# Slots in PSUM named one by one in three dense stages, and two low parts moved behind the gated output's norm

## What is computed

```
for l in range(2):
    q, k, v, r, a_low, u, v_sgu = split(x @ w_in[l])
    y_gla = gla_group(q, k, v, r, a_low, ...)      # ... * silu(r)
    y_sgu = sgu_group(u, v_sgu, ...)
    x = layer_norm(ALPHA * x + concat(y_gla, y_sgu) @ w_out[l])
    x = layer_norm(ALPHA * x + mem_xattn(x, mem, wq, wk, wv, wo))
    x = layer_norm(ALPHA * x + grouped_moe(x))     # 16 experts, 2 of them for a token
h = rms_norm(x)
proj = h @ w_in_2                                  # q, k, v, z, xbc, dt, gate_a, gate_b
y_a = moba_attention(q, k, v) @ w_out_a
u   = ssd(xbc, dt) * silu(z)
y_b = rms_norm_in_groups(u) @ w_out_b
x = x + (gate_a * y_a + gate_b * y_b) @ w_out_2
x = x + hier_moe(rms_norm(x))                      # 16 experts
x = x + sigmoid(x @ w_ple_gate) * (p @ w_ple_proj)
out = rms_norm(x)
```

## Time and profile before

| | us |
|---|---|
| median of 3 runs | 1660.1 |
| the runs | 1664.85, 1658.19, 1660.1 |
| the profiled execution | 1664.57 |
| its span, first to last instruction | 1662.8 |
| its mean granted TensorE clock | 0.966 of full speed |

### The profile page before, as it was taken

The page is one execution under the profiler, slowest core; times in us unless marked ns, Lnnn a source line. Parts: engine busy times, 40 slices in busy tenths (PEclk is TensorE's granted clock), DMA queues, the critical chain, the costliest instruction groups (busy, mean ns, idle before and its releaser), DMA issues.

```text
span 1662.8 us, 21036 instructions
## 1 busy us (share of the span) xinstructions
PE 1543.1 (93%) x8087; PEld 1296.8 (78%) x8087; DVE 1274.3 (77%) x1594; ACT 1119.2 (67%) x1340; POOL 57.2 (3%) x94
## 2 busy tenths in 40 slices
PE   7999988999997989998999998898998889999976
PEld 5788877888886778976788886787887778888855
DVE  4757458999997476447999998558655689999963
ACT  4544537999994644445999997267453479999952
POOL 5000000000001000000000000000000000000000
PEclk8999999999998999999999999999988999999988
DMA  9345427999996534534999998343533479999950
GB/s 330 124 164 202 152 102 271 391 392 392 393 395 249 173 134 170 204 125 153 377 391 393 393 395 334 121 152 102 172 132 98 162 249 388 392 393 395 394 194 26
DMA packets 176693, 422.75 MB, mean 254 GB/s; under 512 B 7052, under 2 KB 7216, under 8 KB 176576
## 3 DMA queue, kind: packets, MB, share of 16 engines
q1 hardware_dynamic: 172400, 407.92, 67.2%
q0 software_dynamic: 4176, 13.30, 2.4%
HBM read 420.15 MB, written 1.05 MB: 253 GB/s over the span
## 4 chain that ended last, share of the span: by engine, by line
PE 72%; DVE 16%; ACT 7%; issue 4%; DMA 1%; POOL 0%; POOLq 0%; ACTq 0%; DVEq 0%
PE ps L960 14%; DVE w_low L1652 11%; PE ps L986 7%; PE ps L675 5%; PE ps L676 4%; PE ps L680 4%; PE ps L997 4%; ACT w_high L1336 3%; PE ps L722 3%; PE ps L782 3%; PE ps L723 3%; PE ps L969 3%; PE ps L789 3%; PE ps L783 3%; PE ps L727 3%
## 5 line engine op out<-in xcount | busy, mean ns | idle before, releaser
L1652 DVE TENSOR_TENSOR w_low<-raw,w_high 128x1024 fp32r<-128x1024 f32 x588 | 693.9, 1222 | 253.3 <-ACT w_high L1336 250.1
L1336 ACT ACTIVATE w_high<-raw 128x1024 fp32r<-128x1024 f32 x588 | 598.2, 1055 | 334.7 <-PE ps L680 122.9
L986 PE MATMUL ps<-w_high,hT 128*128 128x512 f32 x384 | 154.0, 401 | 0.4
L986 PE MATMUL ps<-w_low,hT 128*128 128x512 f32 x384 | 153.2, 399 | 0.0
L960 PE MATMUL ps<-w_high,x_first 128*128 128x512 f32 x384 | 152.4, 397 | 0.3 <-ACT x_first L1389 0.2
L960 PE MATMUL ps<-w_low,x_first 128*128 128x512 f32 x384 | 150.2, 391 | 0.0
L675 PE MATMUL ps<-w_high,act_high 128*128 128x512 f32 x272 | 111.3, 409 | 6.4 <-DVE w_low L1652 3.6
L1652 DVE TENSOR_TENSOR w_low<-work,w_high 128x1024 fp32r<-128x1024 f32 x96 | 113.1, 1221 | 0.0
L676 PE MATMUL ps<-w_low,act_high 128*128 128x512 f32 x272 | 109.3, 402 | 0.0
L1652 DVE TENSOR_TENSOR w_low<-x_res,w_high 128x1024 fp32r<-128x1024 f32 x90 | 106.0, 1221 | 0.0
L680 PE MATMUL ps<-w_high,act_low 128*128 128x512 f32 x272 | 104.0, 395 | 0.0
(11 more groups left out here) (372 smaller groups left out, 3102.9 us busy)
## 6 DMA issues: line engine op xcount, KB each, us to landing
raw<-in_w_up SPq DMA_DIRECT2D x96, 1024.0 KB, 8.8
raw<-in_w_gate SPq DMA_DIRECT2D x51, 1024.0 KB, 9.0
raw<-in_w_down SPq DMA_DIRECT2D x48, 1024.0 KB, 8.6
work<-in_w_gate SPq DMA_DIRECT2D x45, 1024.0 KB, 8.7
x_res<-in_w_down SPq DMA_DIRECT2D x45, 1024.0 KB, 8.2
raw<-in_w_in SPq DMA_DIRECT2D x44, 1024.0 KB, 6.2
raw<-in_w_out SPq DMA_DIRECT2D x12, 1024.0 KB, 5.0
raw<-in_wk_x SPq DMA_DIRECT2D x8, 1024.0 KB, 5.0
```

Of the source, the lines that this page charges most:

```text
L986: i = pe.matmul(YS[:, b, :], hT[:, k, :], weights(u, 512 * b, 512 * b + 512)[half_w], start=(k + half_w == 0), stop=(k + half_w == FC))
L1336: A(split_unit(n)[0], raw_unit(n), ACT.Copy).then_inc(high_ready, 1)
L1652: V.tensor_tensor(split_unit(n)[1], raw_unit(n), split_unit(n)[0].bitcast(F32), ALU.subtract).then_inc(low_ready, 1)
```

## The change

The round-robin slots are replaced by named ones for the jobs from k0a to pos in each layer of the first kind, and from uT0 to pos in the last block. In a layer, s0 to s3 are the slots of mix_sgu, o0, o1 and r:

| job | slot before, layer 0 (its job before) | slot after, layer 0 (its job before) |
|---|---|---|
| k0a, k0b | 2 (o1), 3 (r) | 0 (mix_sgu), 1 (o0) |
| yT0, yT1 | 0 (mix_sgu), 1 (o0) | 2 (o1), 3 (r) |
| xva | 2 (k1a) | 2 (h0) |
| x1T0, x1T1 | 0 (h0), 1 (h1) | 3 (h1), 0 (k1a) |
| pT0, pT1 | 2 (q1b), 3 (xvb) | 0 (q1a), 1 (s0) |
| xh0, xh1 | 2 (pT0), 3 (pT1) | 0 (pT0), 1 (pT1) |
| x2T0, x2T1 | 3 (xh1), 2 (xh0) | 3 (oT0), 2 (oT1) |

In the last block uT1 goes from slot 1 (ya0) to slot 3 (y3), yb0 and yb1 to the slots of ya0 and ya1, mT1 to slot 3, h0 and h1 to the slots of yb0 and yb1, x1T0 from behind h1 to behind mT1, x1T1 from behind h0 to behind mT0. In layer 1, x2T0 already lay behind oT0 before.

With a `head`, `dense_rows` now begins each of its two slots only as it comes to that token tile. Two low parts (the `split(2)` of VectorE between u's product and its norm) move behind the norm, the read of ya and uT's low parts; ScalarE's two high parts of the same units move behind uT's high parts. No instruction on data is added or taken away.

```diff
+    def plan_in(slots, *names):
+        nonlocal next_slot
+        for name, slot in zip(names, slots):
+            next_slot = slot
+            plan_job(name)
...
-        plan_job(L + "yT0", L + "yT1")
-        plan_dense([cols(a["wk_x"][l], 0, j) for j in range(2)], L + "k0a", L + "k0b")
-        plan_dense([rows(a["w_out"][l], j) for j in range(4)], L + "h0", L + "h1")
-        plan_dense([cols(a["wk_x"][l], 512, j) for j in range(2)], L + "k1a", L + "k1b")
-        plan_job(L + "x1T0", L + "x1T1")
-        plan_dense([cols(a["wv_x"][l], 0, j) for j in range(2)], L + "xva")
-        for b in range(2):
-            plan_dense([cols(a["wq_x"][l], 512 * b, j) for j in range(2)], L + f"q{b}a", L + f"q{b}b")
-        plan_dense([cols(a["wv_x"][l], 512, j) for j in range(2)], L + "xvb")
-        plan_job(L + "s0", L + "s1", L + "pT0", L + "pT1", L + "oT0", L + "oT1")
-        plan_dense([rows(a["wo_x"][l], j) for j in range(4)], L + "xh0", L + "xh1")
-        plan_routing(L, "x2T")
+        s0, s1, s2, s3 = slots_of(L + "mix_sgu", L + "o0", L + "o1", L + "r")
+        plan_dense([cols(a["wk_x"][l], 0, j) for j in range(2)], L + "k0a", L + "k0b", slots=(s0, s1))
+        plan_in((s2, s3), L + "yT0", L + "yT1")
+        plan_dense([rows(a["w_out"][l], j) for j in range(4)], L + "h0", L + "h1", slots=(s2, s3))
+        plan_dense([cols(a["wk_x"][l], 512, j) for j in range(2)], L + "k1a", L + "k1b", slots=(s0, s1))
+        plan_dense([cols(a["wv_x"][l], 0, j) for j in range(2)], L + "xva", slots=(s2,))
+        plan_in((s3, s0), L + "x1T0", L + "x1T1")
+        for b, q_slots in enumerate(((s1, s3), (s0, s2))):
+            plan_dense([cols(a["wq_x"][l], 512 * b, j) for j in range(2)], L + f"q{b}a", L + f"q{b}b", slots=q_slots)
+        plan_dense([cols(a["wv_x"][l], 512, j) for j in range(2)], L + "xvb", slots=(s3,))
+        s_late = SUM_SLOTS[1 - SUM_SLOTS.index(s3)]
+        p_early = s0 + s2 - s_late
+        plan_in((s1, s_late, p_early, s1, s3, s_late), L + "s0", L + "s1", L + "pT0", L + "pT1", L + "oT0", L + "oT1")
+        plan_dense([rows(a["wo_x"][l], j) for j in range(4)], L + "xh0", L + "xh1", slots=(p_early, s1))
+        plan_routing(L, "x2T", (3, 2, 0, 1, 0))
...
-    plan_job("2.uT0", "2.uT1")
-    plan_dense([rows(a["w_out_b_2"][0], j) for j in range(4)], "2.yb0", "2.yb1")
-    plan_job("2.mT0", "2.mT1")
-    plan_dense([rows(a["w_out_2"][0], j) for j in range(4)], "2.h0", "2.h1")
-    plan_routing("2.", "x1T")
+    products, turns_in = slots_of("2.ya0", "2.ya1"), slots_of("2.csb3", "2.y3")
+    plan_in(turns_in, "2.uT0", "2.uT1")
+    plan_dense([rows(a["w_out_b_2"][0], j) for j in range(4)], "2.yb0", "2.yb1", slots=products)
+    plan_in(turns_in, "2.mT0", "2.mT1")
+    plan_dense([rows(a["w_out_2"][0], j) for j in range(4)], "2.h0", "2.h1", slots=products)
+    plan_routing("2.", "x1T", (3, 0, 1, 0, 1))
...
-                for t in range(TT):
-                    begin(names[t])
+                if head is None:
+                    for t in range(TT):
+                        begin(names[t])
...
                         high_made(halves[0] if halves is not None else head[t])
+                        if head is not None:
+                            begin(names[t])
...
-            split(2)
             tiles_high(aux_high, ("2.uT0", "2.uT1"))
-            split(8)
+            split(10)
...
                 V.tensor_tensor(zs[:, t, :], zs[:, t, :], xs[:, t, :], ALU.mult).then_inc(S["u_ready"], 1)
-            split(2)
...
             tiles_low(aux_low, aux_high, ("2.uT0", "2.uT1"))
-            split(8 - TAIL)
+            split(10 - TAIL)
```

More of the change, by code:

```diff
@@ L111, in plan_job, with slots_of, plan_dense @@
             next_slot = (next_slot + 1) % SLOTS
-    def plan_dense(sources, *names):
+    def plan_in(slots, *names):
[3 more added lines that the diff above has]
+            plan_job(name)
+    def slots_of(*names):
+        return [job[name][0] for name in names]
+    def plan_dense(sources, *names, slots=None):
         nonlocal n_units, plain
-        plan_job(*names)
+        if slots is None:
+            plan_job(*names)
+        else:
+            plan_in(slots, *names)
         stream.extend(sources)
@@ L133, in build, with plan_routing @@
     UNITS = 12
-    def plan_routing(L, turned_input):
-        nonlocal next_slot
-        for t in range(TT):
[L138 to L143, removed]
+    def plan_routing(L, turned_input, slots):
+        plan_in(slots, L + turned_input + "0", L + turned_input + "1", L + "routerT", L + "router", L + "pos")
     def gate_at(e):
@@ L211, in build @@
     plan_job("2.y3")
-    plan_job("2.uT0", "2.uT1")
-    plan_dense([rows(a["w_out_b_2"][0], j) for j in range(4)], "2.yb0", "2.yb1")
-    plan_job("2.mT0", "2.mT1")
-    plan_dense([rows(a["w_out_2"][0], j) for j in range(4)], "2.h0", "2.h1")
-    plan_routing("2.", "x1T")
+    products, turns_in = slots_of("2.ya0", "2.ya1"), slots_of("2.csb3", "2.y3")
[4 more added lines that the diff above has]
+    plan_routing("2.", "x1T", (3, 0, 1, 0, 1))
+    assert set(turns_in) == {0, 3}
     plan_moe(a["w_gate_2"][0], a["w_up_2"][0], a["w_down_2"][0])
```

## The result

The changed kernel takes 1635.45 us (median of 4 runs, 1633.67 to 1635.94) against 1661.32 us before (4 runs, 1658.19 to 1664.85): 25.9 us or 1.6% less, ratio 0.9839 with a 95% interval of 0.9824 to 0.9854. The prediction was 1638.0 us in a range of 1631 to 1646. The profiled execution took 1635.94 us with a span of 1634.2 us; before it was 1664.57 and 1662.8.

What follows compares the result with a forecast made beforehand. TensorE, busy 93% of the span, bounds the kernel; dense stages gain only where it idles or runs at half clock. Terms 11.6 + 3.4 + 0.5 - 3.0 + 1.0 + 7.6 + 0.3 + 1.0 = 22.4 us off the 1660.1 median: 1638, range 1631 to 1646.

Steps and rivals of the forecast that it cites:

- k0: k0 after r, both layers: the wait for ScalarE's read and the half clock behind it go, 11.6 us won.
- xva: xva after k1, both layers: the 1.69 us wait for ScalarE's read of k1a goes, 3.4 us won.
- pT1 and oT: Cross part of both layers: 0.5 us won, but one wait of some 3.2 us drops the clock, 3.0 us lost.
- the prediction's other reading: Ahead of oT: turns don't count as busy for the clock gate, so the new pattern costs nothing, 3.0 us better.
- x2T of layer 0: Turning ahead of layer 0's router: 1.8 us of wait won, 0.8 lost to half clock, net 1.0 us.
- The norm: Gated output's norm, last block: norm moved ahead of two low parts, yb starts earlier at full clock, 7.6 us won.
- x1T and pg: Last block: 0.3 us won at x1T; pg0 starts after the read of pp0 alone, 1.0 us won.
- (a): Rival: clock falls for longer at oT twice and at two routers, 10.4 instead of 3.8, 1644 to 1645 us; chance 0.12.
- the clock terms: Half clock expected ahead of oT in both layers, 3.0 us lost, and in layer 0's router, 0.8 us lost.
- (b): Rival at k0: something other than r's slot holds k0 or the turning, 11.6 us missing, 1649.5 us; chance 0.04.
- (c): Rival: expert stages, paced by transfers, give the gain back, near no change, 1655 to 1660 us; chance 0.03.
- (d): Rival: transfer rate in expert stages drops to 376 GB/s or less, slower, about 1671 us; chance 0.02.

Runs made afterwards that it cites:

- the filled wait: Kernel before plus seven idle products between the begins of k0a and k0b, both layers: 1656.27 us against 1661.05.
- the two half kernels: Kernel before with only the norm's order changed, 1654.91 us; kernel before with only the last block's slots and late begin, 1657.03 us; before, 1660.69.

## Why the prediction was right

The measured time lies in the middle of the range, and most terms came out as priced, by the mechanism that was given for them. One did not, and part of the closeness of the total is luck, as said under the base.

**k0** was priced at 11.6 us and gave 3.90 + 2.59 + 3.89 + 1.56 = 11.9. Both halves of the reasoning held by themselves: the wait was the slot's (no bracket in the timeline), and the slow units were the clock's (the filled wait). The turning of y came 5.76 us after k0's start, as the 5.8 said, and just did not wait, with both tiles of y ready at that moment.

**xva** was priced at 3.4 and gave 3.7 in the traces. The experiment that took it back has the two waits of 1.69 us again and 4.0 us between the medians.

**pT1 and oT** is the step that failed, in two places. The prediction said that TensorE would stand still for 3.2 us in one piece. It is 2.25: the prediction let the wait begin where pT0's turns ended and forgot that pT1's own 8 turns, no longer held back, move ahead of it. And it said that the clock would fall behind it, 3.0 us lost; in the changed kernel's trace it stayed at 1.00 in both layers. The gain there is the 0.4 us per layer (0.37 and 0.38) and no loss: this term is 3.2 us better than forecast, and larger than the 2.6 by which the whole forecast was off (1638.0 to 1635.45). But the mechanism isn't wrong, only the certainty. The traces of the experiments show both patterns often enough to count, by the time from oT's start to xh's (6.8 us at full clock, 8.4 to 8.5 after a fall). Behind the single wait of 2.25 us, which six kernels have in two layers each, the clock fell in 4 of 12 places; behind the old pair of 1.25 and 1.16 us, also in six kernels, it fell in 1 of 12. At 1.7 us for a fall that is an estimate of 0.6 us lost per layer against 0.1 before, where the prediction took 1.5 against nothing, so the 0.4 us won and the clock lost about cancel, as the kernel with the old pair in it shows too. That the single wait makes a fall likelier is suggested by 4 against 1, not shown. Nor do the counts bear out the prediction's other reading, that the new pattern costs nothing.

**x2T of layer 0**: the lead grew by 3.71 us at its first idle products and 1.96 of that went again up to the router, as x2T1 hangs on the norm: 1.75 us, as the 1.8 said. The half clock, taken at 0.8 as a middle, came in full, 1.60. In layer 1, where nothing was expected, it went away and gave 1.54. For the two layers together that is 1.7 us, against 1.0. This is not a matter of one execution: with two and seven idle products, layer 0's router fell to half clock in each of the five profiles with the new slots and in none of the five with the old, layer 1's in one of five with the new and four of five with the old. The change moved the fall from one layer to the other. Why layer 1's router, whose waits are nearly the same (1.76 and 1.21 us against 1.45 and 1.20), mostly escapes now is open.

**The norm** was priced at 7.6 us (4.5 for the chain, 1.6 for the slot, 1.5 for the clock) and gave 4.4 + 1.58 + 1.43 = 7.4. The two moved low parts cost nothing, as said: yb took 21.9 us, and an undisturbed product takes 21.8. Order and slots are both needed, as the two half kernels show.

**x1T and pg** were 0.3 and 1.0; the trace has 0.3 (1.95 won at x1T0's first idle products, 1.65 of it given back up to the router) and 0.9. Behind pg's start the changed kernel needs 1634.2 - 1598.75 = 35.5 us to its end and the one before 1662.8 - 1626.12 = 36.7; these 1.2 us were in no term. They are clock again: the wait ahead of pg fell from 3.16 us to 2.25, and the half clock behind it was shorter. The first 10 us of pg, before and after:

```profile
1626.10:1636.10 10.00, 9.98 (x32) 7.99 (x33) 0.00 (x0) 0.00 (x0) 0.00 (x0) 0.69 0.00 0
...
1598.70:1608.70 10.00, 9.95 (x37) 8.12 (x38) 0.73 (x1) 1.60 (x2) 0.00 (x0) 0.83 0.00 0
```

**The rivals.** (a), more clock than thought, did not come: the clock terms were 3.8 us in the sum and near nothing in the trace taken together (-1.60 in one router, +1.54 in the other). It was also priced too dear, at 2.6 us for a fall: at oT and at the routers one cost 1.5 to 1.7. (b) is ruled out by the timeline, (c) and (d) by the table: an expert stage changes the lead by 0.06, 0.18 and 0.33 us.

**The base.** Against the profiled executions the sum is short by 28.6 - 22.4 = 6.2 us: 3.2 of them are oT's clock and wait, 1.2 pg, 0.7 the two routers and x2T, 0.3 each k0 and xva, and the rest is drift of the lead. Against the medians it is short by 3.5 (25.9 - 22.4). Taking the median as the base and not the profiled execution was right: that execution lay 3.2 us above the median of the four runs. The rest of the closeness is luck: the median was 1660.1 when the forecast was made and 1661.32 with the fourth run, and from there the same sum gives 1638.9, a miss of 3.5 us and not of 2.6. Either lies well within the range.

## What to carry to other kernels

A slot is worth giving to a job whose begin would otherwise wait for the read that comes last in a queue; look at TensorE's timeline for idle brackets ended by a read, and ask which slot has been read longest. Price such a wait twice: the time itself and the half clock behind it, which here made up 4.2 of 11.9 us at k0. For the second price take how often the clock fell behind a wait of that length in several executions, and not whether it did in one. When a wait is taken away, write down the whole order of what runs where it stood, instructions that now come earlier too; and a reader's order (reads first, then the silu with its table load) can free a slot as well as a plan of slots can.

## What the runs showed of the hardware

The clock fell to half behind the same wait in some executions and not in others. The counts are over the profiles of all kernels here, one each, in which the wait occurs; a fall is told by the same matmuls taking longer.

| TensorE stands still, us | places | clock fell in |
|---|---|---|
| 1.25 and 1.16, 8 turns between, ahead of oT | 12 | 1 |
| 2.25 ahead of oT | 12 | 4 |
| 3.35 ahead of xb2 | 11 | 10 |
| 3.74 or 3.75 ahead of k0 | 8 | 8 |
| the same, filled with idle products to 0.3 or less | 2 | 0 |
| 4.80 ahead of x2T1, 4.90 ahead of uT0 | 6 | 6 |

So of the single waits seen, those of 3.7 us and more always cost clock and one of 2.25 us in a third of the places. One fall costs 1.5 to 1.7 us here at oT, xb2 and the routers (1.5 to 2.6 at k0), which is near what single runs of one kernel differ by. Three idle products more or less at a place can then not be told from the time alone, while the 24 idle products of the three places together are worth 5 us or more.
